# Hybrid decoder layer on one Trainium2 core: the sample rows' output products in four column quarters, and one wait fewer before the extra expert blocks

## The chip, the cores and the metric

The kernel runs on one core of a Trainium2 chip. The metric is the time of the program on the device in microseconds, the median of three runs. A core has a matrix engine (TensorE, PE in the rows), a vector engine (VectorE, DVE), a scalar engine (ScalarE, ACT), a general engine (GpSimd, POOL) and SyncE (SP), which here only issues DMAs. Each engine runs its own instruction list in order and waits on semaphores of the others. TensorE writes to eight PSUM banks (`pb[0]` to `pb[7]`, 128 partitions by 512 float32 each).

## The reference, cut to what matters

One decoder layer for 512 prompt tokens (and 16 meta tokens) and 8 sample tokens, all in float32. Only two steps matter here.

```
mix = (sigmoid(gate_attn) * A + sigmoid(gate_ssd) * B) @ w_o      # 1024 x 1024
h   = LayerNorm(ALPHA * h + mix)
h   = LayerNorm(ALPHA * h + HierMoE(h))    # top expert group, then top-2 of 8 experts: 32 experts in all
# an expert: (silu(x @ w_gate) * (x @ w_up)) @ w_down, with w_gate, w_up 1024 x 256, w_down 256 x 1024
```

## The kernel before, in words

**Tokens.** The 520 rows that go through the output product are five tiles: tile 0 is the 8 sample rows, tiles 1 to 4 are 128 prompt rows each (`tile_rows(t)` gives 8 or 128).

**The output product (stage "mix").** For each tile t, TensorE transposes the merged rows `Y[:, t]` into banks 0 and 1 (`turn_merged(t)`, eight transposes, L898). ScalarE copies them out into `mT[t % 2]` (`merged(t)`, L1331). TensorE then multiplies (`mix(t)`, by `group`, L575): for each of two halves of the 1024 output columns, eight products over the contraction chunks k, with `mT[t % 2][:, k, 0:r]` as weights (r = 8 or 128 columns of the array) and 512 columns of `w_o` (`wo_a` for k below 4, `wo_b` above) streaming. A float32 product is two instructions in the trace, so `mix(t)` is 32 instructions, whatever r is. VectorE adds the residual and normalises (`norm(t)`, L1818, L1793 to L1805), and afterwards come transposes of `h1` (`turn_h1`, L917), router products (`logits`, L575) and a long chain of small VectorE instructions that routes the tokens.

The list of TensorE is `turn_merged(0)`, `turn_merged(1)`, `mix(0)`, `turn_merged(2)`, `mix(1)`, `turn_merged(3)`, `mix(2)` and so on. The semaphores around it: `mt_mm` (a tile is transposed), `mt_ev` (ScalarE has copied it out), `w_mm` (a tile's products are done), `lnb_dv` (a tile is normalised). `mix(t)` for t of 2 and more also waits for the norm of tile t-2, whose banks it takes again. ScalarE's `merged(t)` for t of 2 and more waits for `w_mm` of t-1, since it overwrites `mT[t % 2]`.

**The experts.** Tokens are packed into half blocks of 64 rows, one expert each, and TensorE takes them two at a time ("main" blocks, `main(b)`, 16 of them): `gate_up` (L989), silu on ScalarE (L1373), product on VectorE (L1942), transposes (L981), `down` (L998). The two experts of a block sit in the two column halves of the array (64 columns of weights each). Weights come through six slots (`wgu`, `wdn`), which SP refills as soon as a block has used them: 2048 KB of gate and up and 1024 KB of down for each expert.

**The extra blocks.** An expert with more than 64 tokens gets further half blocks. They are done in a loop (`Fori`) that stands between main block 12 (the thirteenth, `FIRST` = 13) and main block 13; how often it runs is computed from the routing, and the trace has one pass. In a pass: TensorE transposes the rows in `X[1]` (L966); ScalarE empties bank 0 (`empty_x`, L1369) and VectorE bank 1 (L1939); then `gate_up`, silu (L1393), product, transposes, `down`, and the two halves of `Yout[1]` (L1396 and L1980). GpSimd reads from DRAM the row numbers for the next extra rows (L2181), gathers these rows into `X[1]` (L2148), reads the row numbers for the result (L2187), waits for the result, scatters it (L2152), waits for the gather, and only behind the loop issues the gather of main block 14 into `X[1]` (L2148 again) and then that of block 15.

Main block b leaves its result in `Yout[b % 2]`, and GpSimd scatters it to `scr_y` (L2152), which counts up `yw_out0` for even and `yw_out1` for odd b. In front of the loop ScalarE has the wait that the change takes away:

```
act.wait_ge(S["yw_out0"], 16 * len(range(0, FIRST, 2)))
```

It is the wait for the scatter of main block 12. Inside the loop only `Yout[1]` and `yw_out1` are used; the next writer of `Yout[0]` is main block 14, which waits for `yw_out0` itself.

In the trace's names, `small_f`, `r_f`, `y_f`, `x_f`, `w_f` are five pieces of the on-chip memory, into which all buffers are cut (`mT[0]` is in `y_f`, `mT[1]` in `r_f`, `wo_a` in `x_f`, `wo_b` in `w_f`), and `bank` is PSUM. Line numbers are those of the kernel before.

Of the kernel before, what the change touches and what calls it, by code (L numbers as in the profile page):

```python
# [21 lines left out]
ALU = mybir.AluOpType  # L22
ACT = mybir.ActivationFunctionType
# [3 lines left out]
D = 1024  # L27
# [91 lines left out]
def build(nc, io):  # L119
    ctx = ExitStack()  # L120
    with ctx:
# [23 lines left out]
        def pk(name, rows=P):  # L145
# [93 lines left out]
        gwl = [cut(RW + 4096 * i, KC, 512, whole=rounded) for i in range(2)]  # L239
        gwh = [cut(at, KC, 512, whole=rounded)  # L240
               for at in (RX, RX + 4096, RX, RX + 4096, RYA + 1024, RX + 4096)]
        lg = cut(RY, NT, NG + NE)
        hT = cut(RY, NT, KC, P)
        ssq, rstd = (small[:, 16 + 20 * i:36 + 20 * i].rearrange("p (t g) -> p t g", g=KVH) for i in range(2))
# [77 lines left out]
        for name in ("pack_in x_in x2_in xh_ac xl_dv wh_ac wl_dv rope_in cst_in wr_in wvd_in meta_in cache_in "  # L322
                     "pool_init bf_dv f_mm f_ev conv_dv silu_ac rope_dv rc_pl pm_pl vd_mm vd_ev "
                     "dk_dv dk_ac cs_mm "
                     "tr_mm tr_ev pre_pl cb_mm l_mm l_ac g_dv yd_mm yo_mm st_mm ht_pl h_dv ya_dv dx_pl yx_pl "
                     "bct_mm bct_ev bcs_out ds_ac ds_out dd_in dcol_dv bcg_in0 bcg_in1 bcg_fr sh_ac sh_dv ysx_dv yst_mm yst_ev "
                     "s_mm s_dv p_ac t_mm td_dv ta_ac pv_mm es_dv es_ac o_dv "
                     "sa_dv sa_mm sa_ac "
                     "wt_in0 wt_in1 ln_in ln2_in xt_in wo_in c_mm c_ac c_dv kx_pl xr_in rms_ac mt_mm mt_ev w_mm lnb_dv lg_mm lg_dv rms_dv lv_dv lv_ac "
                     "none_pl id_out hot_dv rt_dv rt_ac rk_mm h1_out tb_in "  # L330
                     "xs_in0 xs_in1 xtr_mm xt_ev gu_mm sg_ac hid_dv "
                     "htr_mm hte_dv dn_mm y_ev ex_mm ex_ac ex_dv ex_in yw_out0 yw_out1 "
                     "gt0 gt1 gt2 gt3 gt4 o_dv2 o_out "
                     "small_out kv_out out_d dve_chain act_chain").split():
            S[name] = sem(name)
# [551 lines left out]
        def pe_mix(pe):  # L887

            pe.wait_ge(S["yst_ev"], 1)
            pe.wait_ge(S["c_ac"], 6 * NT)  # L890

            def turn_merged(t):
                r = tile_rows(t)
                pe.wait_ge(S["c_dv"], 5 * NT + t + 1)
                if t:
                    pe.wait_ge(S["mt_ev"], t)
                for k in range(KC):
                    ins = pe.transpose(pb[k // 4][:, (k % 4) * P:(k % 4) * P + r], Y[0:r, t, k * P:(k + 1) * P],  # L898
                                       ident[0:r, 0:r])
                ins.then_inc(S["mt_mm"], 1)  # L900

            def mix(t):
                r = tile_rows(t)
                pe.wait_ge(S["mt_ev"], t + 1)
                if t >= 2:
                    pe.wait_ge(S["lnb_dv"], t - 1)
                for n in range(2):
                    ins = group(pe, pb[2 + 2 * (t % 2) + n][0:r, :],
                                [(mT[t % 2][:, k, 0:r], (wo_a if k < KC // 2 else wo_b)[:, k % (KC // 2), n * 512:(n + 1) * 512]) for k in range(KC)])
                ins.then_inc(S["w_mm"], 1)  # L910

            def turn_h1(t):
                r = tile_rows(t)
                pe.wait_ge(S["lnb_dv"], t + 1)
                pe.wait_ge(S["mt_ev"], NT + t)
                for k in range(KC):
                    ins = pe.transpose(pb[k // 4][:, (k % 4) * P:(k % 4) * P + r], h1[0:r, t, k * P:(k + 1) * P],  # L917
                                       ident[0:r, 0:r])
                ins.then_inc(S["mt_mm"], 1)

            def logits(t):
                r = tile_rows(t)
                pe.wait_ge(S["mt_ev"], NT + t + 1)
                if t >= 2:
                    pe.wait_ge(S["lg_dv"], t - 1)
                group(pe, pb[6 + t % 2][0:r, 0:NG + NE], [(hT[:, t, k, 0:r], wr[:, k, :]) for k in range(KC)], "lg_mm")

            pe.wait_ge(S["wo_in"], 32)
            pe.wait_ge(S["wr_in"], 16)
            turn_merged(0)  # L930
            turn_merged(1)
            mix(0)
            turn_merged(2)
            mix(1)
            turn_merged(3)
            mix(2)
            turn_merged(4)
            mix(3)
            turn_h1(0)
            turn_h1(1)  # L940
            logits(0)
            mix(4)
            turn_h1(2)
            logits(1)
            turn_h1(3)
            logits(2)
            turn_h1(4)
            logits(3)
            logits(4)
# [375 lines left out]
        def act_mix(act):  # L1325
            act.wait_ge(S["c_dv"], 6 * NT)
            def empty(t, n_turned, dst):
                r = tile_rows(t)
                act.wait_ge(S["mt_mm"], n_turned)
                for n in range(2):  # L1330
                    ins = act.copy(dst(n), pb[n][:, :].rearrange("p (k c) -> p k c", c=P)[:, :, 0:r])  # L1331
                ins.then_inc(S["mt_ev"], 1)

            def merged(t):
                if t >= 2:
                    act.wait_ge(S["w_mm"], t - 1)
                empty(t, t + 1, lambda n: mT[t % 2][:, 4 * n:4 * n + 4, 0:tile_rows(t)])

            def first(t):
                empty(t, NT + t + 1, lambda n: hT[:, t, 4 * n:4 * n + 4, 0:tile_rows(t)])  # L1340
                act.wait_ge(S["lnb_dv"], t + 1)
                a, b = row_cols(t)
                for k in range(2):
                    act.dma_start(tokens_h[k, a:b], h1[0:tile_rows(t), t, :]).then_inc(S["h1_out"], 16)

            for t in range(3):
                merged(t)
            act_root(act, 1)
            merged(3)
            act_root(act, 2)  # L1350
            merged(4)
            act_root(act, 3)
            first(0)
            act_root(act, 4)
            first(1)
            first(2)
            act_root(act, 5)
            first(3)
            first(4)
# [5 lines left out]
        def act_experts(act):  # L1365


            def empty_x(done):
                act.copy(XT[:, 0:4, :].rearrange("p k c -> p (k c)"), pb[0][:, :]).then_inc(S[done], 1)  # L1369

            def main(b, stored, hidden_x):
                act.wait_ge(S["gu_mm"], b + 1)
                act.activation(sg, pb[2 + b % 2][:, 0:DE], ACT.Silu).then_inc(S["sg_ac"], 1)  # L1373
                if hidden_x:
                    act.wait_ge(S["xtr_mm"], b + 2)
                    empty_x("xt_ev")
                act.wait_ge(S["dn_mm"], b + 1)
                if b >= 2:
                    act.wait_ge(S[f"yw_out{b % 2}"], stored)
                act.copy(Yout[b % 2][:, 0:512], pb[6][:, :]).then_inc(S["y_ev"], 1)  # L1380

            act.wait_ge(S["xtr_mm"], 1)
            empty_x("xt_ev")
            for b in range(FIRST):
                main(b, 16 * (b // 2), b + 1 < FIRST)
            extras = act.value_load(table[0:1, 0:1], min_val=1, max_val=NOV)
            before = 16 * len(range(1, FIRST, 2))
            act.wait_ge(S["yw_out0"], 16 * len(range(0, FIRST, 2)))
            with act.Fori(0, extras) as j:
                act.wait_ge(S["ex_mm"], j * 4 + 1)  # L1390
                empty_x("ex_ac")
                act.wait_ge(S["ex_mm"], j * 4 + 2)
                act.activation(sg, pb[3][:, 0:DE], ACT.Silu).then_inc(S["ex_ac"], 1)  # L1393
                act.wait_ge(S["ex_mm"], j * 4 + 4)
                act.wait_ge(S["yw_out1"], j * 16 + before)
                act.copy(Yout[1][0:CAP, 0:512], pb[6][0:CAP, :]).then_inc(S["ex_ac"], 1)  # L1396
            act.wait_ge(S["xtr_mm"], FIRST + 1)
            empty_x("xt_ev")
            extra_stored = act.snap(extras * 16 + before)
            for b in range(FIRST, NPAIR):  # L1400
                assert b < FIRST + 3
                main(b, 16 * (b // 2) if b % 2 == 0 else (extra_stored if b == FIRST else mid_stored), b + 1 < NPAIR)
                if b == FIRST:
                    mid_stored = act.snap(extras * 16 + (before + 16))
# [363 lines left out]
            v.tensor_tensor(yv, yv, own_half, ALU.add).then_inc(S["c_dv"], 1)  # L1768

        def dve_gates(v):  # L1770
            for i in DVE_ORDER[len(Z_TILES):]:
                s, t = GATES[i]
                if i == LATE[0]:
# [598 lines left out]
```

## Time and profile before

| | |
|---|---|
| median of 3 runs | 975.12 us (975.02 to 979.6) |
| the profiled execution | 979.53 us, span 977.8 us |
| TensorE busy | 835.7 us, 85% of the span |
| VectorE, ScalarE, GpSimd busy | 473.9, 261.9, 199.3 us |
| chain that ended last, by engine | TensorE 64%, VectorE 17%, DMA 12% |
| DMA traffic | 182.14 MB |
| mean granted TensorE clock | 0.921 of full speed |

The span runs from the first to the last instruction; the time of the execution is 1.7 us more. The profiled execution is 4.4 us above the median of the three timed runs, and close to the slowest of them. "Chain that ended last" follows the work back from the last instruction, at each step to what released it. In the slices of the page each digit is a fortieth of the span (24.4 us).

### The profile page before, as it was taken

How to read it: one execution, taken by the hardware profiler on the slowest of the kernel's cores; microseconds unless marked ns; L12 is line 12 of the kernel's file. 1: busy time of each engine (PE TensorE's matmuls, PEld its weight loads, DVE VectorE, ACT ScalarE, POOL GpSimd, SP SyncE). 2: the span in 40 equal slices, each digit the busy share in tenths (PEclk: the TensorE clock that was granted, in tenths of full speed). 3: DMA queues.
4: the chain of work that ended last, by engine and by line, in shares of the span. 5: the costliest groups of instructions: out<-in, count | busy, mean ns of one | idle time of the engine just before them, and what ended most of it. 6: DMA issues, size and time to landing. Idle time of an engine off the chain costs nothing.

```text
span 977.8 us, 12187 instructions
## 1 busy us (share of the span) xinstructions
PE 835.7 (85%) x4657; PEld 591.9 (61%) x4657; DVE 473.9 (48%) x1073; ACT 261.9 (27%) x647; POOL 199.3 (20%) x172
## 2 busy tenths in 40 slices
PE   5999798999989896999999899959999887756910
PEld 5997788989878895788888534557333332212300
DVE  5997376656565668793335223471121111101158
ACT  4221453434363247664320110110111110001100
POOL 2774534342013351110000000004111111011000
PEclk9999899999978797999999999969999998978965
DMA  8221211210061122752622490265999999997052
GB/s 306 86 88 29 69 54 35 65 35 32 1 253 54 43 93 108 267 180 117 259 87 86 182 419 2 94 254 218 358 429 421 425 422 424 422 426 308 32 186 86
DMA packets 34474, 182.14 MB, mean 186 GB/s; under 512 B 10997, under 2 KB 11653, under 8 KB 23858
## 3 DMA queue, kind: packets, MB, share of 16 engines
q1 hardware_dynamic: 25488, 159.24, 41.6%
q0 software_dynamic: 7744, 17.86, 5.2%
q10 hardware_dynamic: 1184, 4.26, 1.1%
q8 instruction: 37, 0.61, 0.3%
q14 instruction: 21, 0.16, 0.1%
HBM read 169.03 MB, written 20.77 MB: 194 GB/s over the span
## 4 chain that ended last, share of the span: by engine, by line
PE 64%; DVE 17%; DMA 12%; issue 3%; ACT 1%; SPq 1%; POOL 0%; POOLq 0%; DVEq 0%; ACTq 0%
PE bank L582 9%; PE bank L989 9%; PE bank L583 9%; PE bank L584 9%; DMA x_f<-in_w_gu 8%; PE bank L575 8%; DVE r_f L1445 5%; PE bank L998 4%; PE bank L974 2%; PE bank L766 2%; PE bank L672 2%; PE bank L706 1%; PE bank L798 1%; DMA x_f<-in_conv_state 1%; DMA small_f<-scr_h,x_f 1%
## 5 line engine op out<-in xcount | busy, mean ns | idle before, releaser
L989 PE MATMUL bank<-x_f,r_f 128*64 128x512 f32 x272 | 127.3, 624 | 19.7 <-ACT r_f L1369 11.1
L582 PE MATMUL bank<-r_r,w_r 128*128 128x268 f32 x416 | 126.0, 303 | 10.9 <-DVE w_r L1422 10.3
L583 PE MATMUL bank<-y_r,w_r 128*128 128x268 f32 x416 | 122.7, 295 | 0.0
L584 PE MATMUL bank<-r_r,w_r 128*128 128x268 f32 x416 | 122.5, 295 | 0.0
L583 PE MATMUL bank<-w_r,r_r 128*128 128x512 f32 x240 | 95.8, 399 | 0.0
L582 PEld LDWEIGHTS bank<-r_r,w_r 128*128 128x128 f32 x416 | 82.4, 198 | 15.8 <-DVE w_r L1422 10.3
L582 PE MATMUL bank<-x_r,r_r 128*128 128x512 f32 x200 | 81.5, 408 | 3.8 <-DVE w_r L1729 3.8
L989 PEld LDWEIGHTS bank<-x_f,r_f 128*64 128x64 f32 x272 | 38.4, 144 | 73.5 <-issue 72.5
L583 PEld LDWEIGHTS bank<-y_r,w_r 128*128 128x128 f32 x416 | 82.3, 198 | 0.0
L584 PEld LDWEIGHTS bank<-r_r,w_r 128*128 128x128 f32 x416 | 82.2, 198 | 0.0
L584 PE MATMUL bank<-x_r,w_r 128*128 128x512 f32 x200 | 80.0, 400 | 0.0
L1942 DVE TENSOR_TENSOR y_f<-bank,y_f 128x256 f32<-128x256 f32 x17 | 7.2, 424 | 147.3 <-ACT y_f L1373 127.8
L2039 POOL TENSOR_TENSOR w_r<-w_f,w_r 128x1024 fp32r<-128x1024 f32 x23 | 58.9, 2560 | 78.8 <-ACT w_r L1076 78.8
L989 PE MATMUL bank<-y_f,r_f 128*64 128x512 f32 x160 | 74.8, 623 | 0.0
L1637 DVE CUSTOM_DVE_ANT_0 y_f<-bank,small_f 128x272 f32<-128x272 f32 (+1 forms) x64 | 29.9, 467 | 67.1 <-issue 35.8
L1445 DVE TENSOR_TENSOR r_f<-r_f 32x536 f32<-32x536 f32 x40 | 57.4, 1436 | 2.4 <-ACT r_f L1093 1.1
L583 PEld LDWEIGHTS bank<-w_r,r_r 128*128 128x128 f32 x240 | 46.2, 192 | 10.3
L1213 ACT ACTIVATE y_f<-y_f,r_f 128x272 f32<-128x272 f32 (+1 forms) x64 | 31.7, 496 | 71.7 <-DVE r_f L1639 71.7
L989 PE MATMUL bank<-w_f,r_f 128*64 128x512 f32 x96 | 43.9, 611 | 6.4 <-DMA x_f<-in_w_gu 5.6
L582 PEld LDWEIGHTS bank<-x_r,r_r 128*128 128x128 f32 x200 | 38.3, 192 | 14.6 <-DVE w_r L1729 5.7
L998 PE MATMUL bank<-w_f,y_f 128*64 128x512 f32 x176 | 41.6, 616 | 5.7 <-DVE y_f L1945 5.7
L584 PEld LDWEIGHTS bank<-x_r,w_r 128*128 128x128 f32 x200 | 38.5, 192 | 9.4
(359 smaller groups left out, 1562.4 us busy)
## 6 DMA issues: line engine op xcount, KB each, us to landing
x_f<-in_w_gu SPq DMA_DIRECT2D x17, 2048.0 KB, 27.6
w_f<-in_w_d SPq DMA_DIRECT2D x22, 1024.0 KB, 31.9
y_f<-in_w_gu SPq DMA_DIRECT2D x10, 2048.0 KB, 30.5
w_f<-in_w_f SPq DMA_DIRECT2D x26, 512.0 KB, 3.7
w_f<-in_w_gu SPq DMA_DIRECT2D x6, 2048.0 KB, 25.0
x_f<-in_w_d SPq DMA_DIRECT2D x11, 1024.0 KB, 31.4
w_f<-in_w_t SPq DMA_DIRECT2D x5, 2048.0 KB, 8.0
y_f<-in_state POOLq DMA_DIRECT2D x8, 512.0 KB, 5.1
```

Source lines behind the costliest of these rows:

```text
L575: ins = pe.matmul(out, lhsT, rhs, start=(i == 0), stop=(i == len(pairs) - 1))
L582: pe.matmul(out, ah, bh, start=start, stop=False)
L583: pe.matmul(out, ah, bl, start=False, stop=False)
L584: return pe.matmul(out, al, bh, start=False, stop=stop)
L672: ins = pe.matmul(out[:, r * P:(r + 1) * P], adt[:, c, h:h + 1].broadcast_to((P, P)), upper, start=False, stop=True)
L766: ins = pe.matmul(out, q, k, start=(j == 0), stop=(j == n_products - 1))
L989: ins = pe.matmul(out[half, :], XT[:, k, half], wgu[s][:, k, :], start=(k == 0), stop=(k == KC - 1))
L998: ins = pe.matmul(pb[6 + n][half, :], hidT[:, k, half], wdn[s][:, k, n * 512:(n + 1) * 512], start=(k == 0), stop=(k == last))
L1213: act.activation(pS[i % 8][:, lo:AW], sS[i % 4][:, lo:AW], ACT.Exp, bias=anm[b % 2][:, h:h + 1], accum_out=als[b % 2][:, h:h + 1]).then_in ...
L1445: ins = v.tensor_tensor(swp[32 * o:32 * o + 32, :], r[32 * q:32 * q + 32, :], sinT[32 * q:32 * q + 32, :], ALU.mult)
L1637: link(v.tensor_tensor_reduce(sS[i % 4][:, lo:AW], pb[i % 2][:, lo:AW], mask[:, lo:AW], SCALE, pk("sinks")[:, h:h + 1], ALU.add, ALU.max, ...
L2039: p.tensor_tensor(wfl[i % 4][:, :, :], wf[i % 4][:, :, :], wfh[i % 4][:, :, :].bitcast(F32), ALU.subtract).then_inc(S["wl_dv"], 1)
```

## The change

Two edits that have nothing to do with each other.

**Sample rows.** `mix(0)` goes. In its place `sample_parts` does the same sixteen products, but chunk k goes to columns 32 (k % 4) to 32 (k % 4) + 31 of the array and so to that quarter of the partitions of banks 2 and 3; a quarter sums only two of the eight chunks. For that the weights are 32 columns wide, 8 real ones and 24 of zeros, which ScalarE writes once into `mT[0]` ahead of its first copy (`ACT.Copy` of `wr` with scale 0). The quarters are added by one further product for each half: ScalarE copies both banks into `gpart`, and `sample_sum` multiplies them with `gsum`, a 128 by 8 matrix of ones and zeros that VectorE makes earlier from the identity. `sample_sum` stands behind `turn_merged(2)`, and it, not `sample_parts`, counts up `w_mm`.

**Loop.** ScalarE's wait in front of the loop goes.

```diff
+            def sample_parts():
+                pe.wait_ge(S["mt_ev"], 1)
+                for n in range(2):
+                    for k in range(KC):
+                        j = k % 4
+                        ins = pe.matmul(pb[2 + n][SROW * j:SROW * (j + 1), :], mT[0][:, k, 0:SROW],
+                                        (wo_a if k < KC // 2 else wo_b)[:, k % (KC // 2), n * 512:(n + 1) * 512],
+                                        start=(k < 4), stop=(k >= 4))
+                ins.then_inc(S["sp_mm"], 1)
+
+            def sample_sum():
+                pe.wait_ge(S["sp_ac"], 1)
+                for n in range(2):
+                    ins = pe.matmul(pb[2 + n][0:NSAMP, :], gsum, gpart[:, 512 * n:512 * (n + 1)], start=True, stop=True)
+                ins.then_inc(S["w_mm"], 1)
...
             turn_merged(1)
-            mix(0)
+            sample_parts()
             turn_merged(2)
+            sample_sum()
             mix(1)
...
             def merged(t):
-                if t >= 2:
+                if t == 0:
+                    act.wait_ge(S["wr_in"], 16)
+                    act.activation(mT[0][:, :, NSAMP:SROW], wr[:, :, 0:SROW - NSAMP], ACT.Copy, scale=0.0)
+                if t == 2:
+                    act.wait_ge(S["sp_mm"], 1)
+                    act.copy(gpart[:, 0:512], pb[2][:, :])
+                    act.copy(gpart[:, 512:1024], pb[3][:, :]).then_inc(S["sp_ac"], 1)
+                if t > 2:
                     act.wait_ge(S["w_mm"], t - 1)
                 empty(t, t + 1, lambda n: mT[t % 2][:, 4 * n:4 * n + 4, 0:tile_rows(t)])
...
             before = 16 * len(range(1, FIRST, 2))
-            act.wait_ge(S["yw_out0"], 16 * len(range(0, FIRST, 2)))
             with act.Fori(0, extras) as j:
...
         def dve_gates(v):
+            v.tensor_reduce(gsum, ident.rearrange("p (j c) -> p c j", j=4)[:, 0:NSAMP, :], AX, ALU.add)
             for i in DVE_ORDER[len(Z_TILES):]:
```

How TensorE's list stands at the start of the stage "mix". Before, from the transposes of tile 1 to the first products of tile 1 (a row is an instruction or a run of equal ones; a float32 product is one row entry here):

```order
L898 MATMUL bank<-small_f,y_f 128x128 [waits mt_ev,c_dv]
L898 MATMUL bank<-small_f,y_f 128x128 x7
L575 MATMUL bank<-x_f,y_f 8x512 [waits mt_ev]
L575 MATMUL bank<-x_f,y_f 8x512 x3
L575 MATMUL bank<-w_f,y_f 8x512 x4
L575 MATMUL bank<-x_f,y_f 8x512 x4
L575 MATMUL bank<-w_f,y_f 8x512 x4
L898 MATMUL bank<-small_f,y_f 128x128 [waits mt_ev,c_dv]
L898 MATMUL bank<-small_f,y_f 128x128 x7
L575 MATMUL bank<-x_f,r_f 128x512 [waits mt_ev]
```

The same place in the changed kernel, whose lines are numbered one to twenty-odd higher:

```order
L899 MATMUL bank<-small_f,y_f 128x128 [waits mt_ev,c_dv]
L899 MATMUL bank<-small_f,y_f 128x128 x7
L908 MATMUL bank<-x_f,y_f 32x512 [waits mt_ev]
L908 MATMUL bank<-x_f,y_f 32x512 x3
L908 MATMUL bank<-w_f,y_f 32x512 x4
L908 MATMUL bank<-x_f,y_f 32x512 x4
L908 MATMUL bank<-w_f,y_f 32x512 x4
L899 MATMUL bank<-small_f,y_f 128x128 [waits mt_ev,c_dv]
L899 MATMUL bank<-small_f,y_f 128x128 x7
L916 MATMUL bank<-small_f 8x512 [waits sp_ac]
L916 MATMUL bank<-small_f 8x512
L576 MATMUL bank<-x_f,r_f 128x512 [waits mt_ev]
```

The sixteen products stay where they were, 32 rows of output wide instead of 8, and two products with a wait for ScalarE have come in between the transposes of tile 2 and the products of tile 1.

ScalarE's list at the same place, before: the copies of tiles 0, 1 and 2, then the first root of the norm.

```order
L1331 COPY y_f<-bank 128x4x8 [waits mt_mm,c_dv]
L1331 COPY y_f<-bank 128x4x8
L1331 COPY r_f<-bank 128x512 [waits mt_mm]
L1331 COPY r_f<-bank 128x512
L1331 COPY y_f<-bank 128x512 [waits mt_mm,w_mm]
L1331 COPY y_f<-bank 128x512
L1323 ACT_TABLE_LOAD
```

And in the changed kernel:

```order
L1355 ACTIVATE y_f<-small_f 128x8x24 [waits wr_in,c_dv]
L1349 COPY y_f<-bank 128x4x8 [waits mt_mm]
L1349 COPY y_f<-bank 128x4x8
L1349 COPY r_f<-bank 128x512 [waits mt_mm]
L1349 COPY r_f<-bank 128x512
L1358 COPY small_f<-bank 128x512 [waits sp_mm]
L1359 COPY small_f<-bank 128x512
L1349 COPY y_f<-bank 128x512 [waits mt_mm]
L1349 COPY y_f<-bank 128x512
L1341 ACT_TABLE_LOAD
```

Three instructions have come in: the zeros ahead of the first copy, and the two copies of the quarters ahead of the copies of tile 2.

## Rows read from the trace of the kernel before

**Rows 1.** The page, busy tenths of TensorE and of the DMA engines, 40 slices

```profile
PE   5999798999989896999999899959999887756910
...
DMA  8221211210061122752622490265999999997052
```

**Rows 2.** Stretches: busy PE, PEld, DVE, ACT, POOL; granted clock, DMA share, GB/s

```profile
553.50:557.40 3.90, 3.44 (x11) 1.88 (x12) 0.01 (x1) 1.35 (x4) 0.00 (x0) 0.56 1.00 412
557.40:570.30 12.90, 12.90 (x32) 2.54 (x30) 0.00 (x0) 0.00 (x0) 0.00 (x0) 1.00 1.01 426
...
668.00:675.00 7.00, 6.98 (x32) 2.64 (x32) 0.00 (x0) 1.11 (x1) 4.33 (x6) 1.00 0.15 52
...
758.00:853.00 95.00, 78.20 (x348) 29.12 (x346) 12.81 (x24) 9.46 (x19) 12.13 (x12) 0.93 1.01 423
```

**Rows 3.** TensorE's timeline, start of the output products: start, us, instruction

```profile
553.96 1.94 PE L898 MATMUL bank<-small_f,y_f 128*128 128x128 f32 x8 [2.09 <-ACT y_f L1331]
555.83 4.24 PE L575 MATMUL bank<-x_f,y_f 128*8 128x512 f32 x8
...
570.30 1.09 PE L898 MATMUL bank<-small_f,y_f 128*128 128x128 f32 x8
571.23 3.60 PE L575 MATMUL bank<-x_f,r_f 128*128 128x512 f32 x8
```

**Rows 4.** The chain that ended last, output products: start, us, what

```profile
552.82 0.70 DVE y_f L1768
...
571.39 13.73 PE bank L575 x32
```

**Rows 5.** ScalarE's copies of L1331, 550 to 560: ns min/median/max

```profile
L1331 ACT COPY y_f<-bank x2: 186/188/191, 553.5 to 553.6; 128x32 f32<-128x32 f32 x2
L1331 ACT COPY r_f<-bank x2: 586/588/591, 555.9 to 556.4; 128x512 f32<-128x512 f32 x2
```

**Rows 6.** TensorE's timeline where 32 column products run (sample attention)

```profile
365.83 0.64 PE L845 MATMUL bank<-x_f,r_f 128*32 128x128 f32 x16 [0.44 <-DVE y_f L1554]
...
391.49 0.64 PE L866 MATMUL bank<-w_f,r_f 128*32 128x256 f32 x8
```

**Rows 7.** VectorE's timeline: a norm's first step and the loop's copy, with their waits

```profile
599.77 1.28 DVE L1818 SCALAR_TENSOR_TENSOR r_f<-r_f,bank 128x512 f32<-128x512 f32 x2 [8.86 <-PE bank L575]
...
860.32 0.69 DVE L1939 COPY r_f<-bank 128x512 f32<-128x512 f32 x1 [1.36 <-PE bank L966]
```

**Rows 8.** The chain that ended last, expert blocks

```profile
688.82 6.87 PE bank L989 x32
...
802.19 41.62 DMA x_f<-in_w_gu
...
859.82 10.58 DMA scr_y<-r_f,x_f
870.58 0.59 ACT r_f L1369
...
885.71 0.69 DVE y_f L1980
...
888.45 11.02 DMA small_f<-scr_h,x_f
899.51 1.97 PE bank L966 x8
```

**Rows 9.** GpSimd's timeline around the loop

```profile
872.48 0.99 POOL L2148 DMA_INDIRECT small_f<-scr_h,x_f  x1 [9.50 <-DMA x_f<-scr_id]
873.47 0.57 POOL L2187 DMA_DIRECT2D x_f<-scr_id  x1
887.19 0.95 POOL L2152 DMA_INDIRECT scr_y<-y_f,x_f  x1 [13.15 <-DVE y_f L1980]
```

**Rows 10.** DMA issues, us to landing: those of 873 to 880, then of 834.6 to 836

```profile
x_f<-scr_id POOLq DMA_DIRECT2D x1, 0.2 KB, 8.0
...
y_f<-in_w_gu SPq DMA_DIRECT2D x1, 2048.0 KB, 41.1
```

More of the change, by code:

```diff
@@ L241, in build @@
                for at in (RX, RX + 4096, RX, RX + 4096, RYA + 1024, RX + 4096)]
+        gsum, gpart = cut(C1 + D, NSAMP), cut(C1, D)
         lg = cut(RY, NT, NG + NE)
@@ L328, in build @@
                      "sa_dv sa_mm sa_ac "
-                     "wt_in0 wt_in1 ln_in ln2_in xt_in wo_in c_mm c_ac c_dv kx_pl xr_in rms_ac mt_mm mt_ev w_mm lnb_dv lg_mm lg_dv rms_dv lv_dv lv_ac "
+                     "wt_in0 wt_in1 ln_in ln2_in xt_in wo_in c_mm c_ac c_dv kx_pl xr_in rms_ac mt_mm mt_ev sp_mm sp_ac w_mm lnb_dv lg_mm lg_dv rms_dv lv_dv lv_ac "
                      "none_pl id_out hot_dv rt_dv rt_ac rk_mm h1_out tb_in "
```

## The prediction

> **What bounds the kernel now.** I read the slices of the page first, then the chain that ended last, then each engine's timeline at the two places of the change. In the slices [rows 1] the reader sees TensorE at nine in slices 16 to 25 but one (391 to 635 us), which hold the gates and the output products, and the DMA engines at nine in slices 28 to 35 (684 to 880 us). So TensorE's list is the bound of the first place, and weights arriving are the bound of most of the expert stage: the chain has a DMA of 41.62 us there that waits for nothing but its place in the queue [rows 8], and the DMA share is 1.01 at 423 GB/s from 758 to 853 us [rows 2].
>
> The question for the first edit is then whether microseconds saved at 560 us live through a stage that is bound by DMA. From 668 to 675 the DMA engines are nearly idle, share 0.15 at 52 GB/s [rows 2]. The stream of weights starts when the first expert block has freed its slots (SP waits for `gu_mm`), at 675, and that block follows the output products through the router. It is not pinned to the clock on the wall; it moves with TensorE. So I pass the first gain on in full.
>
> **First edit, step by step.** I measure from the start of the sample products, 555.83, to the start of tile 1's products, 571.23 [rows 3]: 15.4 us before. In the changed kernel that stretch is made of:
>
> - The zeros. They stand behind ScalarE's wait for VectorE's last gate step (ends 552.82 + 0.70 [rows 4]) and in front of the copy that releases TensorE's transposes of tile 1, so they are on the path. A copy takes 188 ns at 32 elements a partition and 588 ns at 512 [rows 5]; in between, 192 elements give 0.188 + 160 x 0.400 / 480 = 0.32 us. Bounds: 0.19 and 0.59.
> - The sixteen products, 32 instructions. One after another they take 13.73 / 32 = 0.429 us each with 128 columns of weights [rows 4], and with 8 they are no faster: 15.4 - 1.09 us for the 32. The nearest row for quarters is the sample attention: 8 instructions of 256 columns, four quarters in turn, in 0.64 us, the last one's tail included, and 16 of 128 columns also in 0.64 [rows 6]. Serially, 256 columns at half of 0.429 would make 8 x 0.214 = 1.72 us, and 128 columns 16 x 0.107 = 1.72 us. 1.72 / 4 = 0.43, and 0.21 for the tail: four at a time. Here that is 8 x 0.429 = 3.43 us, and 0.2 of tail.
> - The clock. From 553.5 to 557.4 the granted clock averages 0.56, so mostly the 1.2 GHz level, after the pauses behind the last gate products, and from 557.4 it is 1.00 [rows 2]. The first eight instructions took 4.24 us instead of 3.60 [rows 3]. I take the same 0.6 us again, because TensorE's work before it is unchanged. If the low level lasted over all of the products, it would be 3.4.
> - The sum's wait. ScalarE copies two banks (588 ns each, overlapping a little, so 1.1 us [rows 5]) after the last product; with 0.1 us for each handover, 1.3 us. The transposes of tile 2 (1.09 us [rows 3]) lie inside this time and were outside before. TensorE pauses some 0.2 us.
> - The sum: two products, four instructions, 4 x 0.429 = 1.72 us.
>
> Together 0.32 + 3.43 + 0.2 + 0.6 + 1.3 + 1.72 = 7.6 us, a gain of **7.8 us**. Quarters that ran only in pairs, as the expert products do (32 instructions in 6.87 us [rows 8]), would make 6.9 of the 3.4 and leave 4.4. Serial quarters would make it 2.5 us of loss.
>
> The Trainium skill, "TensorE: Matmul & The Clock Gate", section "Measured speedup vs the span model", speaks for less: packing of four row tiles was measured there at 3.07 times, of three column tiles at 2.38. By 3.07 the products would be an estimated 4.5 us and the gain 6.8. The rows of this case give four at once apart from a tail that is paid once for a group, and I go by them.
>
> The rest of the first edit costs nothing. VectorE's `gsum` is one small reduction among the gate steps, where TensorE is at nine [rows 1]; laid bare it would be a few tenths of a microsecond, as the smallest copy of [rows 5]. ScalarE's two extra copies delay that of tile 2, which `mix(2)` needs only 13.7 us later. The norm of tile 0 must be done before `mix(2)` as well; of a tile's 14.8 us (13.73 and 1.09) VectorE waits 8.86 [rows 7], so the norm is some 6 us. If that cover were gone, TensorE would wait for `lnb_dv` at 577 us.
>
> **Second edit.** The scatter of block 12 is issued at 859.82 and lands 10.58 us later; ScalarE's copy follows at 870.58 [rows 8]. Without the wait it goes when VectorE makes its own copy of the same transposes, at 860.32 [rows 7]: **10.3 us earlier**. Are the weights there? A later load, of block 13, was asked for at 834.8 and took 41.1 us to land [rows 10], at 875.9. Behind the extra expert's gate and up the queue has five loads up to that one, three of 2048 KB and two of 1024, together 8.4 MB or 20 us at 423 GB/s [rows 2]; so the extra expert's are there at some 856. That holds. The extra block's result would be ready at 885.71 + 0.69 - 10.3 = 876.1, rather less, since TensorE has no long pause behind it.
>
> But GpSimd stands behind it. It has to read the row numbers for the result before it can scatter. It asks at 873.47 [rows 9] and gets them 8.0 us later, at 881.5 [rows 10], and nothing in that part hangs on ScalarE: the gather at 872.48, in front of it, waited for a read of row numbers [rows 9], and that one for the transposes alone. From a landing to the next issue it needs 0.8 us, as from VectorE's copy (886.4) to the scatter at 887.19. So the scatter goes at 882.3 instead of 887.19, **4.9 us earlier**, and with it the gather of block 14, which is next on the chain (888.45, 11.02 us) and which TensorE's transposes wait for at 899.51 [rows 8]. Block 13's `gate_up` fills that time and needs its own weights at 875.9, just when it can start. Of 10.3 us, 4.9 arrive; the rest becomes a pause of TensorE in front of block 14. I keep 0 and 10.3 as the bounds. A gather at 883.5 lies in a busier DMA stretch, but its 11.02 was already among weights.
>
> Sum: 7.8 + 4.9 = 12.7 us. The profiled execution would go from 979.53 to 966.8. It lies 4.4 us above the median, and I take the difference to the median: 975.12 - 12.7 = **962.4 us**.
>
> **Rivals.**
>
> 1. Quarters overlap less than four at a time. For it: here four instructions read four different 512-column streams, twice to four times as long as those of [rows 6]. Against it: those show no loss. Gain 4.4 and 4.9, time 965.8. Chance 0.12.
> 2. The second edit gives nothing: the read of the row numbers or the gather takes 5 us longer, as they share the engines with the weights of the loop's second half, now asked for 10 us earlier. Time 967.3. Chance 0.12.
> 3. The second edit gives its 10.3 us in full, because the row numbers land early; then 957.0. Against it: 8.0 us in a full queue. Chance 0.06.
> 4. The first gain is lost in the weight stream, if it does not shift. Time 970.2. Against it is the share of 0.15 [rows 2]. Chance 0.06.
> 5. Slower. The low clock: the quarters are a short burst, then comes a pause, and if TensorE stayed at 1.2 GHz through `mix(1)` and `mix(2)`, each full-speed microsecond costs another, 2 x 13.7 = 27.5 us [rows 4], time 989.9. It decides for slower by 0.5% from 12.7 + 4.9 = 17.6 us of such work. Against it: the clock rose at 557.4 in unbroken work [rows 2], and the only new pause is 0.2 us. Chance 0.02.
>
> The forecast itself, both gains within 2 us, has 0.62; its own range is 960.4 to 964.4.
>
> **The numbers.** A measurement of this kernel tells about 0.5%, 4.9 us, from no change. Rivals 1 and 2 reach 967.3; one of the three runs before was 4.5 us above the median, so I put the upper end at 969.5, and the lower at 957.5, on the edge of rival 3. Rivals 1, 2, 3 and most of 4 are still faster by over 0.5%; a combination of 1, 2 or 4 ends within it: faster 0.93, same 0.05, slower 0.02.
>
> **What would show it.** In the changed profile: 32 instructions of L908 in about 4.2 us (right) or 7 to 14 (rival 1, serial); one pause of 0.2 us in front of L916; tile 1's products starting some 7.2 us after L908 began; the start of the full DMA stretch earlier by 7.8. In the loop: ScalarE's L1394 beside VectorE's copy, TensorE's `gate_up` 10 us before where it was, GpSimd's scatter released by its row numbers, not by VectorE, and a TensorE pause of some 10 us in front of block 14's transposes, released by the gather. Wrong would be: the gather's landing above 13 us, a clock of 0.5 behind 558 us, or a wait for weights in the extra block.

## The result

The changed kernel takes 963.87 us, median of four runs (961.8 to 966.54), against 975.07 (974.77 to 979.6) before, measured on the same chip: a ratio of 0.9886, 95% interval 0.9863 to 0.9909, faster by 11.1 us with bounds of 8.9 and 13.4. (The ratio and its interval are worked out from all the runs and not from the two medians, which are 11.2 us apart.) The forecast was 962.4. The profiled execution went from 979.53 to 966.54, span 977.8 to 964.8, so 13.0 us there.

The page after, first its span, then the slices of TensorE and of the DMA engines, to be held against [rows 1]:

```profile
span 964.8 us, 12198 instructions
...
PE   5999798999989896999999899959999897874910
...
DMA  8221211111053122663632193265999999998152
```

TensorE has the same valley in slice 26 and the DMA engines the same row of nines; a slice is now 24.1 us. Nothing changed its kind. Stretch by stage:

| place | before, us | after, us | earlier by |
|---|---|---|---|
| first sample product | 555.83 | 556.18 | -0.35 |
| first product of tile 1 | 571.23 | 563.32 | 7.9 |
| pick of expert block 1 (behind block 0's gate and up, start of the full weight stream) | 675.11 | 666.18 | 8.9 |
| gate and up of block 12, released by weights | 843.95 | 834.81 | 9.1 |
| scatter of block 12 | 859.82 | 851.86 | 8.0 |
| scatter of the extra block | 887.19 | 874.67 | 12.5 |
| transposes of block 14 | 899.51 | 887.07 | 12.4 |
| end of the span | 977.8 | 964.8 | 13.0 |

Three steps of this table come from neither edit but from the granted clock. The 80 instructions of the first block's pick took 12.83 us at 0.71 after and 13.96 at 0.65 before, which makes 7.9 into 8.9. The gate and up products of block 12 go the other way, 9.92 against 8.74, and the `down` products of block 14 took 4.50 against 5.07. Together that is some 0.5 us of the 13.0.

**The quarters.** A quarter is 32 columns of the array. TensorE's timeline after, where [rows 3] stood before:

```profile
554.30 1.94 PE L899 MATMUL bank<-small_f,y_f 128*128 128x128 f32 x8 [2.34 <-ACT y_f L1349]
556.18 1.56 PE L908 MATMUL bank<-x_f,y_f 128*32 128x512 f32 x8
557.56 1.03 PE L908 MATMUL bank<-w_f,y_f 128*32 128x512 f32 x8
558.42 1.03 PE L908 MATMUL bank<-x_f,y_f 128*32 128x512 f32 x8
...
560.24 1.09 PE L899 MATMUL bank<-small_f,y_f 128*128 128x128 f32 x8
561.51 1.88 PE L916 MATMUL bank<-small_f 128*8 128x512 f32 x4 [0.18 <-ACT small_f L1359]
563.32 3.70 PE L576 MATMUL bank<-x_f,r_f 128*128 128x512 f32 x8
```

A group of eight instructions starts every 0.86 us once the clock is up, which is 0.107 us each where one behind the other takes 0.429: four at a time. The reader also sees the one new pause, 0.18 us ahead of the sum (L916), released by ScalarE's second copy. ScalarE's timeline there, for [rows 5]:

```profile
553.64 0.36 ACT L1355 ACTIVATE y_f<-small_f 128x192 f32<-128x192 f32 x1 [2.40 <-DVE y_f L1792]
...
560.38 0.59 ACT L1358 COPY small_f<-bank 128x512 f32<-128x512 f32 x1 [3.03 <-PE bank L908]
560.87 0.59 ACT L1359 COPY small_f<-bank 128x512 f32<-128x512 f32 x1
```

**The loop.** GpSimd's timeline after, for [rows 9]:

```profile
851.86 1.00 POOL L2177 DMA_INDIRECT scr_y<-r_f,x_f  x1 [18.18 <-DVE r_f L1987]
854.44 0.60 POOL L2206 DMA_DIRECT2D x_f<-scr_id  x1 [1.58 <-issue]
864.71 0.99 POOL L2173 DMA_INDIRECT small_f<-scr_h,x_f  x1 [9.67 <-DMA x_f<-scr_id]
865.70 0.57 POOL L2212 DMA_DIRECT2D x_f<-scr_id  x1
874.67 0.95 POOL L2177 DMA_INDIRECT scr_y<-y_f,x_f  x1 [8.40 <-DMA x_f<-scr_id]
```

The last row is the one to compare. Its releaser was VectorE's copy of the result after 13.15 us; now it is the read of the row numbers. VectorE had that copy done at 866.62 (its row is 865.94, 0.68), 8 us before. ScalarE's copy of the loop's first transposes now stands beside VectorE's, both at 852.37, and nothing waits for weights in the extra block. The chain that ended last says the same with its two DMAs, where [rows 8] had the scatter:

```profile
854.44 9.45 DMA x_f<-scr_id
...
865.70 8.02 DMA x_f<-scr_id
...
875.92 11.10 DMA small_f<-scr_h,x_f
887.07 1.97 PE bank L984 x8
```

TensorE then waits 11.2 us in front of block 14.

### The profile page after: what moved, and what is told of

Same layout as the page of the kernel before. It is cut to its first block, busy times and chain, and to the rows that moved or that the text cites. A ratio compares the mean times of both kernels' runs of the same rounds, so it can differ in the third digit from the quotient of the medians.

```text
span 964.8 us, 12198 instructions
## 1 busy us (share of the span) xinstructions
PE 825.7 (86%) x4661; PEld 589.0 (61%) x4661; DVE 474.2 (49%) x1074; ACT 263.2 (27%) x650; POOL 199.3 (21%) x172
## 4 chain that ended last, share of the span: by engine, by line
PE 63%; DVE 17%; DMA 13%; issue 3%; ACT 1%; SPq 1%; POOL 0%; POOLq 0%; DVEq 0%; ACTq 0%
PE bank L583 9%; PE bank L585 9%; PE bank L584 9%; PE bank L1007 9%; PE bank L576 6%; DVE r_f L1469 5%; DMA x_f<-in_w_gu 4%; PE bank L1016 4%; DMA y_f<-in_w_gu 3%; PE bank L992 2%; DMA x_f<-scr_id 2%; PE bank L767 2%; PE bank L673 2%; PE bank L707 1%; PE bank L799 1%
## 5 line engine op out<-in xcount | busy, mean ns | idle before, releaser
L583 PE MATMUL bank<-r_r,w_r 128*128 128x268 f32 x416 | 126.0, 303 | 10.8 <-DVE w_r L1446 10.3
L583 PEld LDWEIGHTS bank<-r_r,w_r 128*128 128x128 f32 x416 | 82.5, 198 | 15.7 <-DVE w_r L1446 10.3
L584 PEld LDWEIGHTS bank<-w_r,r_r 128*128 128x128 f32 x240 | 46.2, 192 | 10.3
```

The costliest lines, as they stand in the source:

```text
L583: pe.matmul(out, ah, bh, start=start, stop=False)
L584: pe.matmul(out, ah, bl, start=False, stop=False)
```

## The experiments

Ratios are to the kernel before, timed between the runs of each; its medians in the three sets were 975.24 (the first four experiments), 975.45 and 975.29 us. Where a gain in us stands beside a ratio it is worked out from the ratio. The difference of the two medians can be up to 1.3 us off that, within the interval.

### The quarters alone

```diff
             before = 16 * len(range(1, FIRST, 2))
+            act.wait_ge(S["yw_out0"], 16 * len(range(0, FIRST, 2)))
             with act.Fori(0, extras) as j:
```

(against the changed kernel)

> The changed kernel with ScalarE's wait for the scatter of block 12 put back, so only the column quarters are left of the change. My account: tile 1's products start 7.9 us earlier, the full DMA stretch starts as much earlier, and 8.0 us arrive at the end: 967.1 us. TensorE again pauses some 10 us between the loop's transposes and its gate_up. Rival (the weight stream does not shift and takes the gain back): 975 us, with longer waits for in_w_gu in blocks 9 to 12. Second rival (the quarters' gain is worth more than the trace shows, because of the clock): 965 or less.

Measured: 970.09 us, ratio 0.9934 (0.991 to 0.9957), so 6.4 us, bounds 4.2 and 8.8. The gain passes through the weight stream, so that rival falls, and so does the second one, which needs over 10 us. The interval holds the 8.0 of the account, near its upper end; the medians are only 5.2 us apart. The stream did shift. In the chain that ended last the pick of block 1 stands at 669.47, where it was 675.11 before, and block 12's wait for weights ends at 838.12 against 843.95, so 5.6 us of lead at the start of the stream are 5.8 at its end:

```profile
669.47 9.32 PE bank L992 x80
...
838.12 8.52 PE bank L1007 x32
```

TensorE's timeline of its profiled execution, and the stretch's busy times with the granted clock in the third column from the right:

```profile
557.68 1.93 PE L908 MATMUL bank<-x_f,y_f 128*32 128x512 f32 x8
559.39 1.90 PE L908 MATMUL bank<-w_f,y_f 128*32 128x512 f32 x8
561.09 1.06 PE L908 MATMUL bank<-x_f,y_f 128*32 128x512 f32 x8
...
566.02 3.70 PE L576 MATMUL bank<-x_f,r_f 128*128 128x512 f32 x8
```

```profile
557.60:561.00 3.40, 3.40 (x18) 0.79 (x20) 0.00 (x0) 1.07 (x2) 0.00 (x0) 0.52 1.08 455
561.00:562.90 1.90, 1.90 (x20) 0.39 (x12) 0.00 (x0) 0.00 (x0) 0.00 (x0) 0.97 0.98 414
```

In this execution the products ran at the 1.2 GHz level for 3.4 us instead of about one, and took 5.3 us instead of 4.1: the same code at another granted clock. From the first sample product to tile 1's it is 8.3 us here and 7.1 above, against 15.4 before. And the gates ahead of it, which no edit touches, ended over 2 us later than in the two executions above; in two of the executions below they ended over 2 us earlier. This execution is the slowest of the seven, 973.33 us, so it does not show how much of either sits in the 6.4.

### The loop's wait alone

The kernel before without ScalarE's wait:

```diff
-            act.wait_ge(S["yw_out0"], 16 * len(range(0, FIRST, 2)))
```

> The kernel before with only ScalarE's wait taken away. My account: GpSimd's reads of the row numbers let 4.6 of 10.3 us through (27.4 us from the scatter of block 12 to the scatter of the loop become 22.8): 970.5 us, and with the column quarters alone it adds up to the whole change. Rival (the two edits help each other): 973 or more here. Rival (all of the wait arrives): 964.8 us.

Measured: 972.34 us, ratio 0.9963 (0.9943 to 0.9984), 3.6 us, bounds 1.6 and 5.6. All three accounts' numbers were about a run's spread apart; the interval leaves out 964.8, and no more. GpSimd's timeline shows the place itself:

```profile
859.73 1.00 POOL L2151 DMA_INDIRECT scr_y<-r_f,x_f  x1 [17.39 <-DVE r_f L1961]
...
883.03 0.95 POOL L2151 DMA_INDIRECT scr_y<-y_f,x_f  x1 [8.71 <-DMA x_f<-scr_id]
```

From scatter to scatter 23.3 us, released by the read, against 27.4 before: 4.1. In the times, the 3.6 of this edit and the 6.4 of the quarters make 10.0, and the whole change measured 11.1: they add up within their intervals.

### The row numbers from on chip, without and with the wait

GpSimd's own copies of one column replace both reads from DRAM. The column numbers may reach one past the table in the last of sixteen possible passes, where the gathered rows are not used, so the view is one wider. Both row numbers are now made ahead of the gather; what that order is worth by itself is the next experiment's question.

```diff
+        rows_more = cut(RX + 17040, NHALF + 1).bitcast(I32)
...
-                p.dma_start(extra_at[0]... id_column[bass.ds(j + (NE + 1), 1)] ...).then_inc(S["tb_in"], 16)
-                p.wait_ge(S["tb_in"], j * 32 + 48)
-                gather(X[1][0:CAP, :], extra_at[0][0:CAP, :], "ex_in", p.snap(bounds[0] + 1))
                 p.wait_ge(S["yw_out1"], j * 16 + before)
-                p.dma_start(extra_at[1]... id_column[bass.ds(j + NE, 1)] ...).then_inc(S["tb_in"], 16)
-                p.wait_ge(S["tb_in"], j * 32 + 64)
+                p.tensor_copy(extra_at[0][0:CAP, :], rows_more[0:CAP, bass.ds(j + (NE + 1), 1)]).then_inc(S["xr_pl"], 1)
+                p.tensor_copy(extra_at[1][0:CAP, :], rows_more[0:CAP, bass.ds(j + NE, 1)]).then_inc(S["xr_pl"], 1)
+                p.wait_ge(S["xr_pl"], j * 2 + 2)
+                gather(X[1][0:CAP, :], extra_at[0][0:CAP, :], "ex_in", p.snap(bounds[0] + 1))
```

> The changed kernel, with the loop's two reads of row numbers from DRAM replaced by two copies of one column each by GpSimd, out of the table of all row numbers that is on chip anyway. My account (GpSimd's reads, 9.4 and 8.0 us to landing, one behind the other, hold the scatter): the loop's gather goes some 9 us earlier, the scatter goes 0.8 us behind VectorE's copy of the result, at some 867.4 instead of 874.67, the gather of block 14 7.2 us earlier, and all of it arrives: 956.6 us. Rival (the gathers themselves, or the weights of blocks 14 and 15, hold it): 961 to 964 us, with the scatter early but TensorE's transposes of block 14 released at 885 or later, or a wait for in_w_gu or in_w_d in block 14.

> The same, with ScalarE's wait for the scatter put back: the reads are gone, the wait stays. My account: with the wait the result is the later of the two, the reads end well before it, so taking them away gives nothing: 967.1 us, as with the column quarters alone, and the scatter is released by VectorE's copy. Rival (the reads also load the queue that the scatters and gathers share, so they cost by themselves): 962 to 965 us.

Measured: without the wait 958.26 us, ratio 0.9821 (0.9797 to 0.9844); with it 968.62 us, ratio 0.9926 (0.9904 to 0.9949). So taking the reads away is worth 5.6 us (958.26 against the 963.87 of the changed kernel, measured in another set; 6.3 by the ratios) where the wait is gone, and 1.5 us (968.62 against 970.09, inside the intervals) where it stands. Read the other way, taking the wait away is worth 10.4 us without the reads (968.62 against 958.26, in one set, far outside the intervals), which is all of the 10.3 that the wait took, and about 4 with them. That is the crossing that the account asked for: each of the two hides the other. GpSimd's timeline without the wait:

```profile
848.58 0.99 POOL L2178 DMA_INDIRECT scr_y<-r_f,x_f  x1 [13.16 <-DVE r_f L1988]
850.69 0.18 POOL L2208 COPY x_f<-x_f 64x1 int32 x1 [1.12 <-issue]
850.82 0.17 POOL L2209 COPY x_f<-x_f 64x1 int32 x1
851.81 1.00 POOL L2174 DMA_INDIRECT small_f<-scr_h,x_f  x1 [0.82 <-POOL x_f L2209]
864.11 0.93 POOL L2178 DMA_INDIRECT scr_y<-y_f,x_f  x1 [11.30 <-DVE y_f L2006]
```

and of the same with it:

```profile
876.62 0.93 POOL L2179 DMA_INDIRECT scr_y<-y_f,x_f  x1 [23.61 <-DVE y_f L2007]
```

Scatter to scatter is 15.5 us in the first, 27.9 in the second. In the first, 7.3 of the 22.8 us of the changed kernel are gone, as expected. Of these 5.6 reach the transposes of block 14, since the gather ahead of them took 12.79 us instead of 11.10:

```profile
865.35 12.79 DMA small_f<-scr_h,x_f
```

TensorE's pause in front of these transposes is down from 11.2 to 2.6 us, at 878.18. This is the fastest kernel of the study.

### Both reads at the top of the loop

The changed kernel with the second read moved ahead of the first one's wait and of the gather.

> The changed kernel with both reads of row numbers issued one behind the other at the top of the loop, before the gather, instead of one after the other's landing. Account: the second read no longer stands behind the gather, it lands 1 to 2 us behind the first (some 866), so the loop's scatter is released by VectorE's copy of the result, 7 us earlier than in the changed kernel. But the loop also waits for its own gather, which now goes 1 to 2 us later and takes 7.8 us, before it lets the gather of block 14 go; so that one moves by only 1 to 2 us and the time hardly, 961 to 964 us. Rival (GpSimd's only binding wait was the second read): the gather of block 14 goes 7 us earlier and the time is 957 us.

Measured: 961.86 us, ratio 0.9869 (0.9846 to 0.9892), inside the account's range and away from the rival's 957.

```profile
849.43 0.59 POOL L2207 DMA_DIRECT2D x_f<-scr_id  x1 [1.64 <-issue]
...
861.73 1.00 POOL L2173 DMA_INDIRECT small_f<-scr_h,x_f  x1 [11.13 <-DVE y_f L2005]
863.03 0.96 POOL L2177 DMA_INDIRECT scr_y<-y_f,x_f  x1 [0.30 <-issue]
870.71 1.04 POOL L2173 DMA_INDIRECT small_f<-scr_h,x_f  x1 [6.72 <-DMA small_f<-scr_h,x_f]
```

The scatter goes early and the gather of block 14 still waits 6.72 us for the loop's own gather, as the account had it; it is 23.9 us behind the scatter of block 12 (846.79), against 24.1 in the changed kernel. (The releaser named at 861.73 is the one that came last by the profile; the reads landed at the same moment.) The second read was not the only binding wait.

### All sixteen products in one quarter

```diff
-                        j = k % 4
+                        j = 0
...
-                                        start=(k < 4), stop=(k >= 4))
+                                        start=(k == 0), stop=(k == KC - 1))
```

> The changed kernel with all sixteen sample products in the first quarter of the array, summed there over all eight chunks; the other three quarters of the banks hold what was there, so the sample rows of the output are not the reference's. Same instructions, same weights of 32 columns, same copies and sum. My account (the gain is that four quarters work at once): 32 x 0.429 = 13.7 us and the clock's 0.6 instead of 4.1 us, the stretch up to tile 1's products some 17.9 us, 2.5 us more than in the kernel before, and with the loop's gain a time of 963.9 + 10.2 = 974 us. Rival (the 32-column form is cheaper by itself): the 32 instructions in under 10 us and a time of 970 us or less.

Measured: 974.91 us, ratio 0.9991 (0.9977 to 1.0005), no gain left. The trace still has one pass of the loop.

```profile
555.59 4.88 PE L908 MATMUL bank<-x_f,y_f 128*32 128x512 f32 x8
...
570.69 1.09 PE L899 MATMUL bank<-small_f,y_f 128*128 128x128 f32 x8
```

The 32 instructions take 15.1 us, against 4.06: having 32 columns instead of 128 is worth nothing, the quarters at once are worth a factor of 3.7 (4.0 where the clock is up, 0.429 against 0.107 us an instruction). From the first sample product to tile 1's it is 18.2 us against the 17.9 counted, and the loop's gain pays for what that is more than 15.4.

### Runs of one quarter: two products in a row, then four

```diff
-                        j = k % 4
+                        j = k // 2
...
-                                        start=(k < 4), stop=(k >= 4))
+                                        start=(k % 2 == 0), stop=(k % 2 == 1))
```

> The changed kernel with the sixteen sample products in the same number and shape, but two products in a row go to the same quarter (chunks 0 and 1 to the first, 2 and 3 to the second, and so on) instead of the quarters in turn. If the four at a time come from products of different quarters standing next to each other in the list (my account): two products of one quarter run behind each other, four instructions of 0.43 us, and only the last of them overlaps the first of the next quarter, so 32 - 7 = 25 steps of 0.43 us, 10.7 us instead of 3.4, and the kernel is some 7 us slower than the changed one: 970.5 to 971 us. Rival (the engine takes instructions of a free quarter past those of a busy one): 4.1 us for the 32 instructions as in the changed kernel, 963.9 us.

Measured: 963.59 us, ratio 0.9886 (0.9866 to 0.9907), as the changed kernel. The account fell. The weights that TensorE loads (PEld in the rows), in order of time:

```profile
555.91 0.14 PEld L908 LDWEIGHTS bank<-x_f,y_f 128*32 128x32 f32 x2 [0.33 <-issue]
555.94 0.13 PEld L908 LDWEIGHTS bank<-w_f,y_f 128*32 128x32 f32 x1
...
556.77 0.19 PEld L908 LDWEIGHTS bank<-x_f,y_f 128*32 128x32 f32 x2 [0.64 <-issue]
556.80 0.19 PEld L908 LDWEIGHTS bank<-w_f,y_f 128*32 128x32 f32 x2
```

Weights for `x_f` (chunks 0 to 3, quarters 0 and 1) and for `w_f` (chunks 4 to 7, quarters 2 and 3) are loaded within 0.06 us of each other at the start, and the next step again has two of each. In the list, eight instructions of `x_f` stand ahead of the first of `w_f`. So the first of `w_f` runs ahead of instructions that stand before it and wait for their quarter.

For the next one the products were sorted by quarter over both halves, eight instructions of one quarter in a row:

```diff
-                for n in range(2):
-                    for k in range(KC):
-                        j = k % 4
+                for j in range(4):
+                    for n, k in ((0, 2 * j), (0, 2 * j + 1), (1, 2 * j), (1, 2 * j + 1)):
...
-                                        start=(k < 4), stop=(k >= 4))
+                                        start=(k % 2 == 0), stop=(k % 2 == 1))
```

> The changed kernel with the sixteen sample products sorted by quarter over both halves: four products, eight instructions, of one quarter in a row. After the run with two products in a row, where all four quarters still started together, my account is that the engine takes instructions of a free quarter past those of a busy one over at least 24 places of its list: 4.1 us again (5.3 with a low clock) and 963.9 us. Rival (it looks ahead over a few instructions only): with eight in a row the quarters start one after the other, 8 to 12 us, and 968 to 972 us.

Measured: 969.91 us, ratio 0.9947 (0.9925 to 0.997). The account formed after the first of the two falls, and the rival's times came:

```profile
552.97 0.14 PEld L907 LDWEIGHTS bank<-x_f,y_f 128*32 128x32 f32 x2 [0.17 <-issue]
553.70 0.17 PEld L907 LDWEIGHTS bank<-x_f,y_f 128*32 128x32 f32 x1 [0.59 <-issue]
554.55 0.17 PEld L907 LDWEIGHTS bank<-x_f,y_f 128*32 128x32 f32 x1 [0.68 <-issue]
555.41 0.17 PEld L907 LDWEIGHTS bank<-x_f,y_f 128*32 128x32 f32 x1 [0.68 <-issue]
556.26 0.19 PEld L907 LDWEIGHTS bank<-x_f,y_f 128*32 128x32 f32 x3 [0.68 <-issue]
556.84 0.12 PEld L907 LDWEIGHTS bank<-x_f,y_f 128*32 128x32 f32 x2 [0.39 <-issue]
```

The first quarter works alone for four steps, then two side by side for three or four, then one again, and so on; 10.5 us from the first product to the transposes of tile 2. A fixed look-ahead over the list, as the rival had it, does not fit both runs: in the first, an instruction 12 places down started with the first one, and here one 8 places down waited for four steps. One account does fit both: the list is handed out in order, a quarter can have about four instructions waiting or at work, and the handing out stops at the first that finds its quarter full. With four in a row nothing ever stops; with eight, the second quarter gets its first one only when four of the first are done. The two runs suggest this and do not prove it: five or six instructions of one quarter in a row were not tried.

## Why the prediction was right, step by step

The mechanisms of both edits were right. How near the sums came is in part luck: the 12.7 us met 13.0 in one pair of executions, with some 0.5 from the clock in it, while the two edits alone gave 6.4 and 3.6 in the times, each below its forecast of 7.8 and 4.9 though within its interval.

- **What bounds the kernel, and that the first gain lives through the weight stream.** Right. The stream's start moved with TensorE (8.9 us, of which 1.1 is the clock in the pick of the first block), and the quarters alone gave 6.4 us at the end. Rival 4 is out.
- **The zeros**, 0.32 us: the first sample products start 0.35 us later, of which some 0.1 was there before ScalarE began (551.34 against 551.25 in the transposes of tile 0), so 0.25.
- **The products**, 3.43 + 0.2 + 0.6 = 4.2 us: 4.06. Rival 1 is out, with the one-quarter run as the other end, 15.1 us. The Trainium skill's factor of 3.07 for four row tiles ("TensorE: Matmul & The Clock Gate", "Measured speedup vs the span model") would have made an estimated 4.9 us of the 15.1; the trace has 3.7 times for four column quarters, so here the measurement decides.
- **The clock's 0.6 us** was 0.5 in this execution and is the least certain term: it was 1.7 us in the execution with the quarters alone, and as much in the one with both reads at the top.
- **The sum's wait and the sum**, 1.3 and 1.72 us: 1.27 (560.24 to 561.51) and 1.81. The pause of 0.2 us: 0.18.
- **ScalarE's wait**, 10.3 us, with GpSimd's reads letting 4.9 through. Right in place and in kind: the scatter's releaser is the read, and 12.5 - 8.0 = 4.5 us arrive in the profile, 4.1 in the execution with only this edit, 3.6 in the times. It was mis-sized by some 0.4: from the first read to the gather it was 10.27 us instead of 10.10, and from the second landing to the scatter 0.95 instead of 0.8. Rivals 2 and 3 are out. The crossing shows what rival 3 lacked: the wait is worth its 10.3 us in full once the two reads are gone.
- **The sum**, 12.7 us: 13.0 between the profiled executions, 11.1 between the timed ones. That the difference of two executions was set against the median of others is where 1.5 us went: see the clock below. Rival 5 did not occur: from 557.56 to 577 the granted clock was 1.00.

## What to carry to other kernels

Here a product with 8 columns of weights took the time of one with 128, 0.429 us an instruction. Cut its contraction into quarters of the array, sum the quarters by one more product with ones, and hide the copy between behind work that was due anyway: 15.4 us became 7.5. Before a wait is taken away, list what the next engine in line waits for besides: of 10.3 us only 4.5 came through two small reads behind one another, and these were worth 5.6 us more once the wait was gone and next to nothing before. A DMA of 64 numbers took 8 to 11 us in these traces, at a DMA share of 1.00 to 1.01; a copy of a column that is on chip already took 0.18 us.

## What the runs showed that was not expected

- **TensorE does not keep its list's order across quarters.** The opening says that each engine runs its list in order; here a product started together with one that stood 12 instructions before it, and ahead of those between them that waited for their quarter. With eight of one quarter in a row most of that was lost (10.5 us instead of 4.1).
- **The granted clock goes with most of the spread of the runs.** Of the 18 runs of the kernel before in the first set the fastest took 972.6 us at a mean clock of 0.929 and the slowest 980.1 at 0.919, with a correlation of -0.82 and some 0.6 us for each 0.001. In the other two sets it was -0.94 and 0.6 (11 runs), and -0.70 and 0.4 (16 runs). A correlation does not say which of the two drives the other; the traces show the same instructions at different levels after the same pause. The gate and up products of block 12 after the wait for weights took 8.74 us before and 9.92 after, as the chain that ended last has them in the two profiles:

```profile
843.95 8.74 PE bank L989 x32
...
834.81 9.92 PE bank L1007 x32
```

These two stretches of the changed kernel after that wait, granted clock in the third column from the right:

```profile
834.80:838.50 3.70, 3.69 (x10) 1.35 (x12) 0.00 (x0) 0.00 (x0) 0.00 (x0) 0.50 1.03 432
838.50:844.80 6.30, 6.22 (x24) 1.79 (x21) 0.00 (x0) 0.04 (x1) 0.00 (x0) 0.84 1.01 425
```

That is why the 9.1 us of lead at 834.81 were 8.0 at the scatter. The profiled execution before, at 0.921, stood 4.4 us above its median; that such stretches made it so is likely and not shown, as no faster execution of that kernel was profiled.
